# Hybrid decoder step: the router's logits with the weights stationary in two column halves, turned back by TensorE

## What is computed

```
mix = concat([attn, conv]) @ w_out + b_out
h = layer_norm(ALPHA * x + mix)
lg = x2d @ w_rg                      # x2d = h, 1024 wide; 4 group logits
g_idx = argmax(lg); p_g = softmax(lg)[g_idx]
le = x2d @ w_re                      # 4 groups x 8 expert logits
top_v, top_i = top_k(le[g_idx], 2)
gate = p_g * softmax(top_v)
expert = g_idx * 8 + top_i
# tokens are sorted by expert; each expert: (silu(x@w1) * (x@w3)) @ w2
y = layer_norm(ALPHA * h + f)
```

## Time and profile before

| what | us |
|---|---|
| median of three runs | 1359.32 |
| the three runs | 1358.72 to 1360.58 |
| the profiled execution | 1360.41 |
| its span in the trace | 1358.6 |
| TensorE busy | 1251.0 (92%) |
| VectorE busy | 735.9 (54%) |
| ScalarE busy | 537.4 (40%) |
| GpSimd busy | 472.9 (35%) |

### The profile page before, as it was taken

How to read it: one execution, slowest core, us unless ns; L and a number is a source line. 1 busy time by engine, 2 the same in 40 slices (tenths; PEclk the granted TensorE clock), 3 DMA queues, 4 the chain that set the end, 5 groups by cost and what they waited for, 6 DMA issues and landing times.

```text
span 1358.6 us, 21260 instructions
## 1 busy us (share of the span) xinstructions
PE 1251.0 (92%) x5579; PEld 599.8 (44%) x5580; DVE 735.9 (54%) x2093; ACT 537.4 (40%) x883; POOL 472.9 (35%) x633
## 2 busy tenths in 40 slices
PE   7999997999999998899999999899999999999910
PEld 3444444666666654545555545333333333333300
DVE  2423433555555564668889888534444444444348
ACT  0000100343444543423333332366666655666544
POOL 5112210000000000345555554354566666665322
PEclk9999998999999999999999999999999999999965
DMA  6265545232212166256666554289899999999686
GB/s 257 91 225 161 179 128 171 76 113 78 65 53 78 55 197 190 91 203 215 218 219 187 156 148 136 76 257 329 274 328 366 328 291 339 322 368 354 193 268 265
DMA packets 91256, 273.41 MB, mean 201 GB/s; under 512 B 14888, under 2 KB 41088, under 8 KB 78038
## 3 DMA queue, kind: packets, MB, share of 16 engines
q1 hardware_dynamic: 73975, 226.53, 46.9%
q0 software_dynamic: 14384, 42.32, 13.1%
q10 hardware_dynamic: 2807, 3.53, 0.8%
HBM read 212.80 MB, written 66.40 MB: 206 GB/s over the span
## 4 chain that ended last, share of the span: by engine, by line
PE 49%; issue 29%; DVE 9%; DVEq 4%; DMA 4%; ACT 1%; POOLq 1%; POOL 1%; SPq 1%; ACTq 0%
PE P L1119 13%; PE bank_S L1141 9%; PE M L1119 6%; PE bank_S L738 4%; PE P L738 3%; PE bank_T L738 2%; PE bank_S L912 2%; DVEq L1709 2%; PE M L738 2%; DMA work<-conv_rows 2%; PE P L912 1%; PE M L1127 1%; DVE route L1714 1%; DMA big<-sum_rows 1%; DVE work L1671 1%
## 5 line engine op out<-in xcount | busy, mean ns | idle before, releaser
L1383 ACT ACTIVATE big<-big 128x2048 f32 x76 | 145.0, 1910 | 122.3 <-issue 82.4
L1119 PE MATMUL P<-big,work 128*64 x416 | 188.0, 595 | 1.9 <-DVE work L1927 1.4
L1120 PE MATMUL P<-big,work 128*64 128x512 f32 x416 | 188.0, 595 | 0.0
L777 PE MATMUL P<-big,work 128*128 128x256 f32 (+1 forms) x512 | 173.2, 494 | 7.3 <-DMA work<-in_xt_prompt 7.3
L2118 POOL DMA_INDIRECT work<-h_rows,piece_idx x148 | 141.9, 959 | 62.9 <-issue 40.4
L1141 PE MATMUL bank_S<-big,work 128*64 x304 | 136.7, 592 | 1.0 <-DVE work L1911 1.0
L1143 PE MATMUL bank_S<-big,work 128*64 128x512 f32 x304 | 136.7, 592 | 0.0
L2034 POOL TENSOR_SCALAR work<-work 128x1 f32<-128x1 f32 (+1 forms) x17 | 3.8, 221 | 369.8 <-DVE work L1592 369.7
L777 PEld LDWEIGHTS P<-big,work 128*128 128x128 f32 x512 | 96.3, 192 | 78.2 <-issue 64.6
L912 PE MATMUL P<-big,work 128*128 128x512 f32 x256 | 115.4, 604 | 0.0
L912 PE MATMUL bank_S<-big,work 128*128 128x512 f32 x256 | 113.8, 598 | 0.0
(11 more groups left out here) (356 smaller groups left out, 2261.0 us busy)
## 6 DMA issues: line engine op xcount, KB each, us to landing
big<-in_w SPq DMA_DIRECT2D x96, 1024.0 KB
work<-in_xt_prompt SPq DMA_DIRECT2D x32, 512.0 KB, 3.8
big<-sum_rows SPq DMA_DIRECT2D x16, 520.0 KB, 8.7
big<-in_toe SPq DMA_DIRECT2D x16, 512.0 KB, 3.3
work<-in_x_prompt SPq DMA_DIRECT2D x16, 512.0 KB, 4.2
h_rows<-work SPq DMA_DIRECT2D x16, 512.0 KB, 2.7
sum_rows<-work SPq DMA_DIRECT2D x16, 512.0 KB, 3.6
out_y_prompt<-big SPq DMA_DIRECT2D x16, 512.0 KB
```

The lines of the kernel that those rows point to most:

```text
L777: last = mm(dst[0:n, 0:c1 - c0], lhs[:, k, :], w_qkv[:, k, c0:c1], start=(k == 0), stop=(k == KD - 1))
L1119: mm(lower, xgT[j][:, k, 0:U], both[:, k], start=(k == 0), stop=(k == KD - 1))
L1120: last = mm(upper, xgT[j][:, k, U:P], w_up[:, k], start=(k == 0), stop=(k == KD - 1))
L1383: fn(w_up.rearrange("p k m f -> p m k f")[:, :, ks, :], src, ACT.Copy).then_inc(s[f"wu{part}_ok"], 1)
```

## The change

The router's weights become the stationary side and the tokens the stream. The sum over the 8 pieces of k is split in two: pieces 0 to 3 go to the column half that writes partitions 0 to 36 of M0, pieces 4 to 7 to the half that writes partitions 64 to 100. So the logits come out turned, with the logit on the partition, as two partial sums. ScalarE copies both to SBUF (`copy_logits`, into a buffer of the attention stage that is free by then and is cleared once), TensorE turns all 101 rows back with one transpose (`turn_logits`, placed after the third of the eight multiplies of the projection's second half), and VectorE adds the two partial sums while it reads them; for the row's sum it stores both parts, which are added later anyway. Three semaphores of the sample's attention become one with three counts, to make room for two new ones.

```
             def router(c):
...
-                for k in range(KD):
-                    last = mm(M0[0:n, 0:NR], hT[:, k, 0:n], wr_v[:, k, :], start=(k == 0), stop=(k == KD - 1))
+                for k in range(KD // 2):
+                    for h in range(2):
+                        kk = k + h * KD // 2
+                        last = mm(M0[h * U:h * U + NR, 128:128 + n], wr_v[:, kk, :], hT[:, kk, 0:n], start=(k == 0), stop=(k == KD // 2 - 1))
                 last.then_inc(s["pe_ro"], 1)
+
+            def turn_logits(c):
+                n = rows_of(OUT_IN[c])
+                after(pe, s["ro_c"], c)
+                tr(M0[0:n, 256:256 + RO], lgT[0:RO, 0:n], ident[0:RO, 0:RO]).then_inc(s["pe_rt"], 1)
...
+                    if k == 3 and between is not None:
+                        turn_logits(between)
...
                 if c <= NT:
-                    project_out(c, 1, "pe_o1")
+                    project_out(c, 1, "pe_o1", c - 2 if c >= 2 else None)
+                if c == NT + 1:
+                    turn_logits(c - 2)
                 if c == NT + 2:
-                    early_product(0, 3, 7)
+                    early_product(0, 3, 4)
+                    turn_logits(c - 2)
+                    early_product(0, 4, 7)
...
+            def copy_logits(c):
+                n = rows_of(OUT_IN[c])
+                after(act, s["pe_ro"], c)
+                after(act, s["pe_rt"], c - 1)
+                for h in range(2):
+                    last = fn(lgT[h * U:h * U + NR, 0:n], M0[h * U:h * U + NR, 128:128 + n], ACT.Copy)
+                last.then_inc(s["ro_c"], 1)
...
                 if 2 <= c + 1 <= NT:
                     swish_conv(c + 1)
+                if 0 <= c - 2:
+                    copy_logits(c - 2)
                 if 0 <= c - 2 and c - 1 != NT:
                     gate_exps(c - 2)
...
             def route_top(c):
                 n = rows_of(OUT_IN[c])
-                after(v, s["pe_ro"], c)
+                after(v, s["pe_rt"], c)
                 after(v, s["ro_e1"], c - 1)
                 if c >= 2:
                     v.wait_ge(s[f"sum_out{c % 2}"], 16 * (c // 2))
-                cp(hsum[c % 2][0:n, 0:1], M0[0:n, NG + NE:NR])
-                cp(lg8[0:n, 0:NG], M0[0:n, 0:NG])
-                cp(le[0:n, :], M0[0:n, NG:NG + NE]).then_inc(s["ro_ev"], 1)
+                low, high = M0[0:n, 256:256 + NR], M0[0:n, 256 + U:256 + RO]
+                cp(hsum[c % 2][0:n, 0:2], M0[0:n, 256 + NR - 1:256 + RO:U])
+                cp(lg8[0:n, 0:NG], low[:, 0:NG])
+                cp(le[0:n, :], low[:, NG:NG + NE])
+                v.drain()
+                tt(lg8[0:n, 0:NG], lg8[0:n, 0:NG], high[:, 0:NG], ALU.add)
+                tt(le[0:n, :], le[0:n, :], high[:, NG:NG + NE], ALU.add).then_inc(s["ro_ev"], 1)
```

More of the change, by code:

```diff
@@ L164 @@
 cn_in0 cn_in1 am_in0 am_in1 xr_in0 xr_in1 xb_ok cstat_ok cnm_ok z_ev pe_z zl_ok zs_ok mix_ok
-pe_o0 pe_o1 o0_ev o1_ev lstat_ok lrs_ok dg_ok lz_ok h_ok h_out0 h_out1 sum_out0 sum_out1 hp_in pe_hT hT_ev pe_ro ro_ev ro_nm ro_e1 ro_d ro_e2
+pe_o0 pe_o1 o0_ev o1_ev lstat_ok lrs_ok dg_ok lz_ok h_ok h_out0 h_out1 sum_out0 sum_out1 hp_in pe_hT hT_ev pe_ro ro_c pe_rt ro_ev ro_nm ro_e1 ro_d ro_e2
 oh_ok pe_rk rk_ev slot_ok sc_out0 sc_out1 last_out s_cache s_row s_vs
-pe_smp sA_ev sm_ok s_p sB_ev sconv_ok
+pe_smp sA_ev sB_ev sV_ok
 early_out tab_build pe_tab eids_ok idx_ok tab_ok tab_in0 tab_in1 tab_in2 tab_in3 tab_in4 tab_in5
@@ L364, in layer @@
         assert FEWEST >= UN and NE * U > EARLY * U
+        RO = U + NR
+        lgT = V[1]
         EARLY_PE = {"turned": (1, 2), "up": (3, 4), "turned_g": (5, 7), "down": (6, 8)}
@@ L866, in sample_piece @@
                 elif step == 4:
-                    pe.wait_ge(s["s_p"], 1)
+                    pe.wait_ge(s["sV_ok"], 3)
                     tr(M0[:, 128:192], Ps, ident[0:64, 0:64]).then_inc(s["pe_smp"], 1)
@@ L876, in sample_piece @@
                 elif step == 6:
-                    pe.wait_ge(s["sconv_ok"], 1)
+                    pe.wait_ge(s["sV_ok"], 1)
                     for c in range(CC):
@@ L900, in project_out_sample, with project_out @@
                 last.then_inc(s["pe_o1"], 1)
-            def project_out(c, half, sem):
+            def project_out(c, half, sem, between=None):
                 n = rows_of(OUT_IN[c])
@@ L1222, in sample_piece @@
                 elif step == 3:
-                    act.wait_ge(s["sm_ok"], 1)
+                    act.wait_ge(s["sV_ok"], 2)
                     fn(Ps, M0[0:64, 128:256], ACT.Exp, bias=s_nm, scale=SCALE, accum_out=s_rs)
@@ L1564, in sample_conv @@
                     last = ts(conv_s[:, c, :], conv_s[:, c, :], cw[:, c, TAPS:TAPS + 1], None, ALU.add)
-                last.then_inc(s["sconv_ok"], 1)
+                last.then_inc(s["sV_ok"], 1)
             def sample_max():
@@ L1572, in sample_max @@
                 v.drain()
-                tt(s_dd, s_nm, s_ns, ALU.subtract).then_inc(s["sm_ok"], 1)
+                tt(s_dd, s_nm, s_ns, ALU.subtract).then_inc(s["sV_ok"], 1)
             def sample_norm():
@@ L1580, in sample_norm @@
                 v.drain()
-                ts(Ps, Ps, s_li, None, ALU.mult).then_inc(s["s_p"], 1)
+                ts(Ps, Ps, s_li, None, ALU.mult).then_inc(s["sV_ok"], 1)
             def conv_stats(c):
@@ L1780, in _ @@
             v.memset(done_u, 0.0)
+            v.memset(lgT, 0.0)
             for c in range(NT + 4):
```

## The result

The changed kernel takes 1420.97 us (median of four runs, 1419.15 to 1423.88), the kernel before 1359.84 us (1358.72 to 1360.58) beside it: ratio 1.0456, 95% interval 1.0439 to 1.0473. It is slower by 61 us. The forecast was 48 us slower, 1407 us, in a range that ends at 1421. By the ratio it is 62 us, which is at the end of the range or just past it. The direction and the mechanism hold, and the size is 13 to 14 us too small. The profiled execution of the changed kernel took 1423.88 us (span 1422.0), 63.5 us more than the profiled one of before.

What follows compares the result with a forecast made beforehand. VectorE was taken to bind by a hair. Twelve rounds at 3.19 us (38.3), 6 for the clock, and 1.7 + 1.4 + 0.5 + 0.4 - 0.3 for other rounds summed to 48 us: 1407 us, range 1393 to 1421.

Steps and rivals of the forecast that it cites:

- What bounds the kernel: Output projection with router: VectorE binds by a hair, 16.75 us a round against 16.5 of TensorE work.
- the copies are not held: Rival: ScalarE has its Sigmoid done by the router's end, leaving 0.34 us a round, 5 us: 1364 us; chance 6%.
- (1) The router: On TensorE, the router falls from 1.71 to about 0.9 us, worth nothing while TensorE waits for VectorE.
- (2) The ring: Logits copies queue behind ScalarE's swish_conv; through VectorE, GpSimd, ScalarE and TensorE, route_top starts 3.69 us later every round.
- (3): VectorE's added work in route_top, two additions and one drained step: 0.34 us per tile, between 0.3 and 0.5.
- (4): On VectorE, L1671, started later, finds GpSimd's addition over and gives 0.84 us back.
- 3.19 us a round: Added time per full round: 3.69 later start plus 0.34 added VectorE work less 0.84 given back.
- (5) The clock: TensorE's clock drops after its idle; ten projection records lose 0.9 to 2.3 us, 1.0 hidden, 0.5 a round taken.
- in full: Rival: the slower TensorE clock costs 1.3 us a round instead of 0.5, the turn 1.3: 1422 us; chance 12%.
- (6) The rounds: Rounds 3 to 14 pay in full; round 2 pays 1.7 us, round 15 1.4, round 16 0.5, the tail 0.4.
- the sum without the clock: Stall with TensorE's slower clock costing nothing: 48 - 6 = 42 us, 1401 us; as a rival, chance 25%.
- Nothing behind takes it back.: After the rounds, the routed stage recovers none of the delay; its first experts' weights are there long before.

Runs made afterwards that it cites:

- half_router: The kernel before with every second product of the router left out (4 of 8): ratio 1.0131, mean round 17.06 us against 17.03.
- copy_first: The changed kernel with ScalarE's two logits copies moved ahead of normal_conv and swish_conv: 1359.87 us, ratio 0.9992 to the kernel before.
- awake: The changed kernel with 13 dummy products of 128 columns on TensorE ahead of the turn of the logits: 1406.67 us, ratio 1.0341.
- conv_early: The changed kernel with SyncE issuing the load of the convolution's rows for tile c+3 ahead of load_x(c+2): ratio 1.0391 to the kernel before.
- copy_middle: The changed kernel with ScalarE's two logits copies placed between normal_conv and swish_conv: 1384.67 us, ratio 1.0184 to the kernel before.
- best: The changed kernel with one logits copy ahead of normal_conv, TensorE adding the halves, conv_stats ahead of route_slot and its rows loaded earlier: ratio 0.9896.

## Where the prediction was right and where it fell short

The prediction's points by its own numbers, with what stands behind them:

- **What bounds the kernel.** Right. half_router's saving went into idle; copy_first has rounds of 16.74 us with VectorE end to end. But VectorE's unbroken row of instructions holds two waits for GpSimd, and the prediction saw only the one at L1671. Nor did it draw from it that work put ahead of that wait is hidden: where the copies are not held it charged the additions with 5 us (1364 us), and gave half of that case's 6% to their being hidden. copy_first took 1359.87.
- **(1) The router.** 0.9 us was the estimate; the router and the next record start 1.00 us apart. Worth nothing, and it was.
- **(2) The ring.** `route_top` starts 3.76 us later against `add_half` (4.35 us behind the start of L1648, where it was 0.59 before); the forecast said 3.69. Every hand-over is as described, and copy_first removes it all. From the Sigmoid's end to `route_top` it is 0.97 us (684.63 to 685.60) where the sum had 0.91; 0.55 of it are the copies (estimate 0.45).
- **(3), (4).** From its first to its last instruction `route_top` takes 3.57 us for 4.09 before, 0.52 less; the sum had 0.84 less 0.34, 0.50. L1700 takes 0.23 as foretold. That the 1.07 was a wait on GpSimd and not the instruction's own cost is shown by the matching ends above. The rule that was cited for it from the Trainium skill (SBUF — State Buffer, Who interferes with whom), that one of the two is blocked until the other's instruction is over, agrees with these ends. There the Trainium skill exempts an instruction with one SBUF input only outside the two-port modes; that L1671 runs in such a mode no trace shows. The two additions with one input in PSUM paid nothing, as cited: in copy_first they take 0.16 and 0.18 us in the middle of GpSimd's addition, as in the changed kernel without one.
- **3.19 us a round.** awake gives 3.24.
- **(5) The clock: the step that failed.** "0 to 1.3 us a round are paid. I take 0.5." The term was too small: 6 us in all, where awake prices it at 14.3 us (15.6 by the ratios, 18.2 between the two traces), 1.1 to 1.4 a round. The ten records lose 1.3 to 3.0 us (5.8 to 7.46 us in rounds 2 to 14), where the forecast, from the two stretches in the earlier trace rows, had 0.9 to 2.3. With the 1.0 that is hidden, the rival called "in full" is the nearer one, though the turn it puts at 1.3 took 0.97. The step also looked at one engine only. It asked when VectorE wants the second half-sum and not what else comes late behind a late TensorE: the rows for `conv_stats`. By conv_early, loading them earlier gives back some 9 of the 14 us by itself. Neither the prediction nor its rivals name these rows, though SyncE's queue could have been read for them.
- **(6) The rounds.** With the clock up, the loss is 46 us by awake's ratio of 1.0341, where the sum without the clock had 42. In awake's trace 40.7 us lie between the transposes (foretold for the 12 full rounds and round 15: 39.4), 2.5 between the first projection record of the stage and the first transpose (40.98 against 38.50 us; 1.7 foretold), and 2.7 behind the last transpose (0.9 foretold).
- **"Nothing behind takes it back."** Right: 533.9 us behind the last transpose against 530.3.

So 61 us are 46.8 (ring and additions; forecast 42) and 14.3 (clock, and what it makes late; forecast 6). The mechanism was right and the clock's term mis-sized. The result lies at the upper end of the range, which the forecast reached only with an allowance for what it had missed.

## What to carry to other kernels

A cheap step that is put behind another task in an engine's queue inherits everything that task waits for. Follow the queue back, and if the chain passes through the engine that will wait, the delay comes back every round; here the same step cost 62 us behind two tasks that wait, 25 us between them (copy_middle), and nothing ahead of both (copy_first). When a stall is added to TensorE, price the slower clock behind it too, and then list the transfers whose issue hangs on TensorE's progress. Two neighbouring instructions that always end together on VectorE and GpSimd mark time that can be filled: moving 0.8 us of work there, together with an earlier load of its rows, gave 1% of the whole kernel. Useless work on TensorE can keep its clock up, but here it gave back 14 us where one line moved in ScalarE's queue gave back 61.

## What the hardware showed that was not expected

- Thirteen useless products, about 3.2 us of TensorE work a round, made the kernel 14 us faster, because the granted clock stayed at 1.00 (2.4 GHz) instead of a mean of 0.87 over 620 to 760 us.
- The SCALAR_TENSOR_TENSOR form of the penalty waits on GpSimd's addition just as TENSOR_SCALAR does (1.05 and 1.07 us, both 128x4). In the same stretch a TENSOR_SCALAR on 128x1 (0.14 us), a CAST (0.16) and MAX8 (0.17) ran without delay. What tells the two kinds apart was not tried.
- In best the penalty starts behind GpSimd's addition and takes 0.23 us in eleven of the thirteen rounds from 610 to 805 us. In the other two it takes 0.53 and 0.52 us and ends within 0.03 us of the end of an indirect DMA instruction on GpSimd (674.97 and 675.00 in the first). But such an instruction ran beside it in the eleven too. What makes the difference is open.
